# A hybrid streaming encoder step: table stores in pieces, a sparse search three tiles ahead, paired value products, and longer cache rows

## The reference

```
dots  = einsum('bthd,bsd->bths', iq, ik_all) * D_IDX**-0.5        # 8 index heads of 64
score = einsum('bth,bths->bts', iw * H_IDX**-0.5, relu(dots))
score = where(chunk(kpos) <= chunk(qpos), score, -inf)            # chunks of 64 frames
sel   = top_k(score, 256)
logits = q . k[sel] * HEAD_DIM**-0.5 + rel_bias[t5_bucket(kpos[sel] - qpos)]
out_a = softmax(logits) @ v[sel]
```

## Time and profile before

| | us |
|---|---|
| median of 3 runs | 4598.58 (4596.07 to 4610.59) |
| the profiled execution | 4597.5 |
| its span, first to last instruction | 4595.5 |
| projection | 0 to 690 |
| prompt forget | 690 to 1208 |
| prompt sparse | 1208 to 2252 |
| sample index, sample forget | 2252 to 2330, 2330 to 2588 |
| sample sparse | 2588 to 2765 |
| output projection, MLP | 2765 to 3025, 3025 to 4595 |

### The profile page before, as it was taken

The page is one execution under the profiler, slowest core; times in us unless marked ns, Lnnn a source line. Parts: engine busy times, 40 slices in busy tenths (PEclk is TensorE's granted clock), DMA queues, the critical chain, the costliest instruction groups (busy, mean ns, idle before and its releaser), DMA issues. The chain is left out here.

```text
span 4595.5 us, 57429 instructions
## 1 busy us (share of the span) xinstructions
...
## 2 busy tenths in 40 slices
...
GB/s 136 99 136 116 125 127 116 78 62 73 100 69 44 42 21 42 22 12 16 44 213 358 152 154 180 199 185 156 128 148 161 150 156 138 166 127 155 147 166 146
DMA packets 478319, 558.99 MB, mean 122 GB/s; under 512 B 94961, under 2 KB 387841, under 8 KB 473773
## 3 DMA queue, kind: packets, MB, share of 16 engines
...
HBM read 444.79 MB, written 110.36 MB: 121 GB/s over the span
## 5 line engine op out<-in xcount | busy, mean ns | idle before, releaser
L2292 DVE TENSOR_TENSOR w_lo<-w_raw,w_hi 128x2048 fp32r<-128x2048 f32 x192 | 440.1, 2292 | 644.4 <-ACT w_hi L2257 630.2
L2257 ACT CAST w_hi<-w_raw 128x2048 fp32r<-128x2048 f32 x192 | 366.0, 1906 | 569.8 <-PE ps_y L2242 541.6
L2221 PE MATMUL ps_u<-h_hi,w_hi 128*128 128x384 f32 (+1 forms) x1536 | 506.3, 330 | 49.9 <-DMA h_lo<-h2lo 28.2
L2222 PE MATMUL ps_u<-h_lo,w_hi 128*128 128x384 f32 (+1 forms) x1536 | 503.8, 328 | 0.0
L2223 PE MATMUL ps_u<-h_hi,w_lo 128*128 128x384 f32 (+1 forms) x1536 | 503.7, 328 | 0.0
L2240 PE MATMUL ps_y<-w_hi,hid_hi 128*128 128x512 f32 x1088 | 423.5, 389 | 0.5 <-DVE w_lo L2292 0.4
L2242 PE MATMUL ps_y<-w_hi,hid_lo 128*128 128x512 f32 x1088 | 423.4, 389 | 0.0
L2241 PE MATMUL ps_y<-w_lo,hid_hi 128*128 128x512 f32 x1088 | 423.3, 389 | 0.0
L332 PE MATMUL ps_u<-hT_hi,wi_hi 128*128 128x436 f32 (+1 forms) x920 | 342.1, 372 | 46.6 <-DVE o_lo L494 29.5
L333 PE MATMUL ps_u<-hT_lo,wi_hi 128*128 128x436 f32 (+1 forms) x920 | 335.8, 365 | 0.0
L334 PE MATMUL ps_u<-hT_hi,wi_lo 128*128 128x436 f32 (+1 forms) x920 | 335.7, 365 | 0.0
...
## 6 DMA issues: line engine op xcount, KB each, us to landing
w_raw<-in_w_up SPq DMA_DIRECT2D x96, 1024.0 KB, 5.6
w_raw<-in_w_down SPq DMA_DIRECT2D x96, 1024.0 KB, 4.9
k_rows_b<-in_cache_b_k SPq DMA_DIRECT2D x32, 1024.0 KB, 11.9
v_rows_b<-in_cache_b_v SPq DMA_DIRECT2D x32, 1024.0 KB, 14.0
...
```

What stands on the lines that cost most here:

```text
L2221: pe.matmul(out, w_hi[s][:, c], h_hi[:, k, 0:w], start=(k == 0), stop=False)
L2222: pe.matmul(out, w_hi[s][:, c], h_lo[:, k, 0:w], start=False, stop=False)
L2257: act.copy(w_hi[i % 2][:, :], raw[i % RAW][:, :]).then_inc(ev("w_hi"), 1)
L2292: nc.vector.tensor_tensor(w_lo[i % 2][:, :], raw[i % RAW][:, :], w_hi[i % 2][:, :].bitcast(FP32), ALU.subtract)\
```

## The change

It has four parts.

**1. The table is stored in 16 pieces** of 8 copies (128 KB) by SP, each behind the stores of one unit, from unit 0 of block 11 on, in place of the one DMA on GpSimd.

**2. The search of the prompt's sparse phase** is placed anew. Index units of tile t are spread over both groups of tile t-3, `open` and the 8 halvings over both groups of tile t-2, VectorE's 4 halvings go into the even segment of tile t-1 and the rest, now seven single steps, into its odd one. `score` has three buffers, the index queries one buffer in place of two, and a segment has at least 6 entries. The first index head's weighting moves to GpSimd.

**3. The value products go in pairs**: two blocks are issued one behind the other, the even block into array columns 0 to 63 and the odd one into 64 to 127. The two halves of the result are summed by a product with a doubled identity (`join`) that takes the place of the 4 transposes of `finish`.

**4. K and V rows of the sample's sparse phase** are loaded so that partition p gets rows p*16+k, four rows of 512 bytes in a run. The mask is then read with a step of 16 elements.

```
-        REL_AT = 10
+        REL_AT, SPREAD = 10, 8
...
+            def spread_rel(i):
+                rows = slice(i * SPREAD, (i + 1) * SPREAD)
+                sp.wait_ge(ev("rel_out"), 1)
+                sp.dma_start(d["rel_t"][rows, :].rearrange("p (h r) -> h p r", h=HA), rel.unsqueeze(1).to_broadcast([HA, SPREAD, RELW]))\
+                  .then_inc(ev("st_rel"), 16)
...
+                    after = unit_no[step[1], step[2]] - unit_no[REL_AT + 1, 0]
+                    if 0 <= after < P // SPREAD:
+                        spread_rel(after)
...
+            sp.wait_ge(ev("st_rel"), 16 * P // SPREAD)
...
-            pool.wait_ge(ev("rel_out"), 1)
-            pool.dma_start(d["rel_t"][:, :].rearrange("p (h r) -> h p r", h=HA), rel.unsqueeze(1).to_broadcast([HA, P, RELW])).then_inc(ev("sw_st_rel"), 16)
-            pool.wait_ge(ev("sw_st_rel"), 16)
...
-        NQ, NTB, NR, NPT, LAG, FLAG = 3, 2, 3, 3, 2, 4
+        NQ, NTB, NR, NPT, LAG, FLAG, NPOOL = 3, 2, 3, 4, 2, 5, 1
...
-        q_lo = {k: [sb(f"q_lo_{k}{p}", [P, 8, P], F32R) for p in two] for k in KINDS}
+        NBUF = {"index": 1, "head": 2}
+        q_hi = {k: [sb(f"q_hi_{k}{p}", [P, 8, P], F32R) for p in range(NBUF[k])] for k in KINDS}
+        q_lo = {k: [sb(f"q_lo_{k}{p}", [P, 8, P], F32R) for p in range(NBUF[k])] for k in KINDS}
...
-        score = [sb(f"score{i}", [P, SEQ]) for i in two]
+        score = [sb(f"score{i}", [P, SEQ]) for i in range(3)]
...
         ON_ACT = range(8)
-        EARLY = ["open", *ON_ACT]
-        LATE = [*range(8, BISECT), "first", "second"]
+        OPEN = ["least", "most"]
+        LAST = ["count", "below", "top", "take", "top again", "take again", "mask"]
...
-            t = x // 2 + 2
-            index = [("index", t, h, c) for h in range(HI) for c in range(len(index_chunks(t)))] if x % 2 == 0 and t in indexed else []
-            early = [(t, s) for s in EARLY] if x % 2 and t in indexed else []
-            late = ([(t - 1, s) for s in LATE] if t - 1 in indexed else []) + [(t - 1, "mask")] if x % 2 and t - 1 < NT else []
-            n = max(len(scores), len(turns))
+            n = max(len(scores), len(turns), 6)
...
-            for i, a in enumerate(index):
-                new[i * n // len(index)]["qk"].append(a)
...
-            for i, s in enumerate(early):
-                new[i * n // len(early)]["steps"].append(s)
-            for i, s in enumerate(late):
-                new[i * max(1, n - 2) // len(late)]["steps"].append(s)
...
+        def place(kind, items, first, last):
+            for i, item in enumerate(items):
+                ticks[first + i * (last - first) // len(items)][kind].append(item)
+
+        for t in indexed:
+            units = [("index", t, h, c) for h in range(HI) for c in range(len(index_chunks(t)))]
+            if t == indexed[0]:
+                place("qk", units, begin[0], begin[1])
+                place("steps", [(t, s) for s in [*OPEN, *ON_ACT]], begin[1], begin[2])
+            else:
+                first = max(1, 2 * (t - 3))
+                place("qk", units, begin[first] + 2 - (t == indexed[1]), begin[2 * (t - 2)] - 2 + (t == indexed[1]))
+                place("steps", [(t, s) for s in OPEN], begin[2 * (t - 2)], begin[2 * (t - 2)] + 2)
+                place("steps", [(t, s) for s in ON_ACT], begin[2 * (t - 2)] + 2, begin[2 * (t - 1)])
+            place("steps", [(t, s) for s in range(len(ON_ACT), BISECT)], begin[2 * (t - 1)] + 2, begin[2 * (t - 1) + 1])
+            place("steps", [(t, s) for s in LAST], begin[2 * (t - 1) + 1], begin[2 * t] - 1)
+        ticks[begin[1] + 1]["steps"].append((1, "mask"))
...
-                b = n % 2
-                if n >= 2 and kind == "index":
-                    sp.wait_ge(ev("index_scored"), i0[indexed[n - 2] + 1])
-                elif n >= 2:
+                b = n % NBUF[kind]
+                if n >= 1 and kind == "index":
+                    sp.wait_ge(ev("index_scored"), i0[indexed[n - 1] + 1])
+                elif n >= 2 and kind == "head":
                     sp.wait_ge(ev("head_scored"), a0[2 * (t - 1)])
...
+            for a in two:
+                sp.dma_start(join[a * HD:(a + 1) * HD, :], d["consts"][0:HD, C_ID:C_ID + HD]).then_inc(ev("join_in"), 16)
...
-                for x in ((2 * t - 4, 2 * t - 3) if t >= 2 else ()):
-                    store(x)
-            for x in range(NX - 4, NX):
-                store(x)
...
+            def gather(t, h, c):
+                c0, w = index_chunks(t)[c]
+                r = index_unit(t, h, c)
+                pool.wait_ge(ev("relu_out"), r + 1)
+                acc, src, wt = score[t % 3][:, c0:c0 + w], relu[r % NR][:, 0:w], iw[:, t, h:h + 1]
+                if t == indexed[0] and c == 0:
+                    pool.wait_ge(ev("iw_in"), 16)
+                if t - 3 in indexed:
+                    pool.wait_ge(ev("mask_ready"), t - 2)
+                nc.gpsimd.tensor_scalar(acc, src, wt, None, ALU.mult).then_inc(ev("pool_used"), 1)
+
+            for k, tick in enumerate(ticks):
+                if k in begin[:NX:2]:
+                    add_near(begin.index(k) // 2)
+                for t, step in ticks[k - 1]["steps"] if k else ():
+                    if step == "take":
+                        check_bad(t)
+                for a in tick["qk"]:
+                    if a[0] == "index" and a[2] < NPOOL:
+                        gather(*a[1:])
+                if group_ended(k - FLAG - 2) is not None:
+                    store(group_ended(k - FLAG - 2))
...
-                pe.matmul(ps_o[x % 2][0:HD, :], v[:, kb, m * HD:(m + 1) * HD], pT[n % NPT][:, :], start=(kb == 0), stop=(kb == t)).then_inc(ev("weighed"), 1)
+                half = slice(kb % 2 * HD, kb % 2 * HD + HD)
+                pe.matmul(ps_o[x % 2][half, :], v[:, kb, m * HD:(m + 1) * HD], pT[n % NPT][:, :], start=(kb < 2), stop=(kb >= t - 1)).then_inc(ev("weighed"), 1)
...
-                    tr = pe.transpose(ps_f[:, j * HD:(j + 1) * HD], outT[x % 2][:, j * P:(j + 1) * P], ident[0:HD, 0:HD])
-                tr.then_inc(ev("joined"), 1)
+                    mm = pe.matmul(ps_f[:, j * HD:(j + 1) * HD], outT[x % 2][0:r, j * P:(j + 1) * P], join[0:r, :], start=True, stop=True)
+                mm.then_inc(ev("joined"), 1)
...
-                if k >= LAG and ticks[k - LAG]["turn"]:
-                    weigh(*ticks[k - LAG]["turn"])
+                b = ticks[k - LAG]["turn"] if k >= LAG else None
+                if b:
+                    waiting.append(b)
+                    if len(waiting) == 2 or b[1] == groups[b[0]][0]:
+                        for b in waiting:
+                            weigh(*b)
+                        waiting = []
...
-                acc, src, wt = score[t % 2][:, c0:c0 + w], relu[r % NR][:, 0:w], iw[:, t, h:h + 1]
-                if h == 0:
-                    if t == indexed[0] and c == 0:
-                        dve.wait_ge(ev("iw_in"), 16)
-                    ins = nc.vector.tensor_scalar(acc, src, wt, None, ALU.mult)
-                else:
-                    dve.wait_ge(ev("relu_used"), index_unit(t, h - 1, c) + 1)
-                    ins = nc.vector.scalar_tensor_tensor(acc, src, wt, acc, ALU.mult, ALU.add)
-                ins.then_inc(ev("relu_used"), 1)
+                acc, src, wt = score[t % 3][:, c0:c0 + w], relu[r % NR][:, 0:w], iw[:, t, h:h + 1]
+                name, value = gathered(t, h - 1, c)
+                dve.wait_ge(ev(name), value)
+                nc.vector.scalar_tensor_tensor(acc, src, wt, acc, ALU.mult, ALU.add).then_inc(ev("relu_used"), 1)
...
+            def quarter(what, n):
+                rows = d[f"cache_{cache}_{what}"][0, n // 4, :, :, :]
+                if sparse:
+                    rows = rows.rearrange("(p k) h e -> p k (h e)", k=NBLK)
+                else:
+                    rows = rows.rearrange("(k p) h e -> p k (h e)", p=P)
+                return rows[:, (n % 4) * QUARTER:(n % 4 + 1) * QUARTER, :]
+
...
-                        ins = nc.vector.tensor_tensor_reduce(out=out, in0=src, in1=mask[p][:, c0:c0 + w], scale=1.0,
+                        add = mask[p][:, c0:c0 + w]
+                        if w == BANK:
+                            add = mask[p][:, 0:PAST].rearrange("r (p k) -> r k p", k=NBLK)[:, c0 // P:c0 // P + 4, :]
+                            out, src = out.rearrange("r (k p) -> r k p", p=P), src.rearrange("r (k p) -> r k p", p=P)
+                        ins = nc.vector.tensor_tensor_reduce(out=out, in0=src, in1=add, scale=1.0,
```

83 lines of the change are left out of this document (49 added, 34 removed).

## The result

The changed kernel takes 4529.91 us (median of 4 runs, 4513.64 to 4537.76), the kernel before 4597.32 beside it: a ratio of 0.9844, 95% interval 0.981 to 0.9877. It is faster, but by 67 us and not by the 153 forecast, and 4530 lies above the range.

What follows compares the result with a forecast made beforehand. TensorE and VectorE were taken to limit the prompt's sparse stage by turns. Projection -26, prompt's sparse stage -110 (96 + 18 - 4) and sample's rows -19 sum to -155 us, predicting 4444 us; range 4365 to 4520.

Steps and rivals of the forecast that it cites:

- I take .84, midway between .79 and .894: Prompt's sparse stage: VectorE's busy share rises from .77 to .84, so 903 us become 807, 96 saved.
- Rival (b): Prompt's sparse stage: evening out does not help, search steps wait among logits, share stays .77; about 4517 us, chance .12.
- the bound of 34: Projection: most that storing the table in pieces could gain; 34 us lost less 8 for the pieces gave 26.
- the strips of the earlier trace: Value products: four 32-column strips cost what one product costs, so a pair was priced as one, saving 105 us.
- rival (a): Prompt's sparse stage: paired value products follow one another instead of running side by side; about 4513 us, chance .06.
- 1 to 2 us a tile: Index queries with one buffer: 13.4 us to arrive against some 12 until first use; charged nothing, VectorE having other work.
- The last stretch: End of the prompt's sparse stage, TensorE's alone: 23 pairs save 23 us, less joins and chain end 18, bounds 0 and 22.
- The start: Start of the prompt's sparse stage: third index tile's queries load behind the rest; 4 us charged, bounds 0 to 9.
- the wait of 16.62 us: Sample's sparse stage: this first wait halves with longer row runs, 8 us of the 19 us gain forecast there.
- 148 against 283 GB/s: Sample's sparse against forget stage: rate difference read as 512-byte against 2 KB runs, behind the 19 us gain forecast.
- a reduction of 128 elements: Sample's mask: this reduction with a 256-byte step takes 289 ns, no sign of a fee, so strided reads were charged nothing.
- Rival (e): Prompt's sparse stage: GpSimd's queue, with the first index head's multiply, holds ScalarE up; about 4680 us, chance .03.

Runs made afterwards that it cites:

- the control: Changed kernel, still three score banks, with the joined result put in the bank of the value products instead of its own: 4530.95 us, ratio 0.9852.
- the best version: Changed kernel with four score banks, the search's last part in ten steps instead of seven, and index queries loaded earlier: 4456.59 us, ratio 0.9681.

## Why the prediction was wrong

**The step that failed: "I take .84, midway between .79 and .894".** It held that evening out the work would let VectorE, the fullest engine, be busy a larger share. Its share stayed at .769, and 88 us are missing here. The runs make a small table of it, group 0 to 28 in us (the new place with pairs and three banks also took 885.2 and, in the control, 885.6):

| | single products | pairs |
|---|---|---|
| search in its old place | 903.1 | 879.5 |
| search in its new place | 870.7 | 894.8 |
| new place, four banks | 838.9 | 836.5 |

Each of the two parts gains by itself, 23.6 and 32.4 us. Together they should leave 847; they leave 885 to 895. So 38 to 48 us are lost by their meeting, and the prediction had no term for it: the three banks stand in it only as a reason for the share. The runs showed one cause, and a second in part. (1) VectorE's bursts in the search, 3.4 us in the one shown, now stand in front of index units too, and three banks hold three units of two products each, some .4 to .5 us a product; a fourth bank gives 49 to 58 us back (836.5), shorter bursts 14 to 24 (871.0), both 67 to 76 (818.5). (2) With pairs TensorE's work is uneven from entry to entry and its clock falls, .90 to .82 up to group 24; filling the light entries gives 16 to 26 us back (869.3). It stays open whether this is the clock or the unevenness. The clock by itself does not make the loss: in the old order it falls with pairs too, .87 to .82, and they gain 23.6 us. The remedies overlap: after the first the second gives nothing.

With both parts of (1) mended, VectorE's share is nearly what I had forecast: 682 us in 818.5, .83, against 678 in 807. So the share was within reach; that three banks let the kernel reach it was assumed from one good segment (42.01 of 47.0 us), which had no index units in it.

**Rival (b)** had the effect, the share staying at .77, and a time of 4517, 13 us off; its reason, halvings that delay ReLUs, was not tested. What the runs show is the small steps of the search among logits, its other half. That it came within 13 us of the time is in part luck, since it takes the table, the end and the rows at the forecast's figures, and those were off both ways. The trace before had rows that spoke for more than its chance of .12: of the 105.8 us that TensorE already waited for VectorE 102.7 lie in the segments with a search and 3.0 in those with index units, and the change moves half of the index units into the odd segments, where the end of the search stands.

**Part 1** was right in kind and too small: -35.3 and -37.6 against -26, beyond the bound of 34. All the 34 us lost came back, and the 8 charged for the pieces did not come: the DMA share is .63, and from 340 to 420 us ScalarE waits for no store, only for TensorE.

**TensorE's side.** Pairs cost what one product costs, as taken from the strips of the earlier trace rows; rival (a) is out. But the busy time is 657 and not 615. Value products fell from 266.8 to 164.0 us, as forecast. The joins cost 22 us more than the transposes that they replace (36.6 against 14.4), where 16 were charged. The others grew at the lower clock, the two index products from 236.6 to 259.5: I had priced products at the clock that they had. Group 0 to 28, before and now:

```profile
L1091 PE MATMUL ps_o_sp<-pT_sp,v_sp 128*64 128x512 f32 x448 | 266.8, 683 | 8.1 <-ACT pT_sp L1135 8.1
...
L1072 PE MATMUL ps_s_sp<-k_index_sp,q_hi_index_sp 128*128 128x512 f32 (+3 forms) x294 | 123.6, 422 | 66.8 <-DVE cmax_sp L1198 60.8 <-ACT relu_sp L1128 5.5
L1073 PE MATMUL ps_s_sp<-k_index_sp,q_lo_index_sp 128*128 128x512 f32 (+3 forms) x294 | 113.0, 389 | 0.0
```

```profile
L1143 PE MATMUL ps_o_sp<-pT_sp,v_sp 128*64 128x512 f32 x448 | 164.0, 757 | 3.3 <-ACT pT_sp L1196 3.3
...
L1123 PE MATMUL ps_s_sp<-k_index_sp,q_hi_index_sp 128*128 128x512 f32 (+3 forms) x288 | 136.5, 475 | 146.7 <-DVE cmax_sp L1260 99.4 <-issue 26.1 <-ACT relu_sp L1189 20.8
L1124 PE MATMUL ps_s_sp<-k_index_sp,q_lo_index_sp 128*128 128x512 f32 (+3 forms) x288 | 123.0, 433 | 0.0
```

**The one buffer for index queries** has a term in the prediction, 1 to 2 us a tile, that was charged at nothing. In these rows it is the 26.1 us behind `issue`: seven waits of 1.8 to 4.8 us before an index unit, each of which ends .1 us after the last query load of its tile has landed (in one of them it lands at 1741.04 and the product begins at 1741.13). The kernel before has none of them there, the best version still has seven, 30.3 us. No run gives the queries a second buffer again, so what these waits cost the stage is not shown.

**The last stretch** gave 25.1, above the bound of 22: 23 pairs and nothing charged by the joins.

**The start** cost 12.9, not 4. TensorE stood 10.29 us for the queries of tile 3, the second tile that is searched; their last load lands at 1225.90:

```profile
1226.00 0.76 PE L1123 MATMUL ps_s_sp<-k_index_sp,q_hi_index_sp 128*128 128x512 f32 x1 [10.29 <-issue]
```

I had counted the eight loads' own issue and landing, 8 us, but not the 21 loads in front of them, which I had named only as the rest. Asking earlier gave 4.8 back; where the other 8 went is not shown.

**Part 4** gave some 7 us, not 19: the stage takes 136.8, 135.0 and 133.4 us in the three runs without it and 123 to 139 in the 17 with it, 128 in the middle. Of the terms, the wait of 16.62 us did not halve: the second of the two waits for K takes 17.3 us now. The wait for V did shrink, 14.5 to 5.3 us (3.5 to 8.9 in 14 of the 17 runs, 10.7 to 16.3 in the other three), but not as forecast, since V lands later, in 12.9 us where 10.0 stood; what shortened it stays open. Rows of 512 bytes were not what held the loads: with four in a run K lands in 13.1 us, not 12.0. On this the Trainium skill, *DMA: Bandwidth & Descriptors*, section Specifications, had the better answer: 512 bytes are enough for line rate. The trace agrees as far as the landing goes. I had read 148 against 283 GB/s as the rows' doing, but the mask's loads are in the same figure.

The Trainium skill, *SBUF — State Buffer*, section Door 1: The DMA port swizzle, charges a step that leaves a 16-byte line with every access. The trace agrees: 1011 against 690 ns, and 690 again without the step. It shows the strided addition as another instruction, too (`CUSTOM_DVE_ANT_1`), and no run parts the step from that. I had charged none, by a reduction of 128 elements. It costs no time here that the runs can tell: without the step the stage takes 130.5 us.

**Rival (e)** did not come: without GpSimd's multiply the phase takes as long. My price for it, 1.07 us, was too low (1570 ns at 512 wide).
